# Reordering everything ahead of the experts in a two-layer decoder trunk: first loads, projection columns with Pool's mixing, added tensors, 512-wide dense products, routing, and a 0/1 scatter of the experts' results

## The reference, cut to what matters

```python
for l in range(2):
    h = rms_norm(x, mix_norm[l])
    proj = h @ w_in                                   # 3328 columns; 32 more (vres_down) in layer 1
    p_rwkv = token_shift(proj[..., :1792], mu)        # p + (prev - p) * mu; columns r, k, v (512 each), lora (256)
    p_diff = proj[..., 1792:3328]                     # q, k, v of the attention, 512 each
    ...
    y_rwkv = rwkv7_time_mix(p_rwkv, ...)              # delta-rule recurrence over 256 tokens, 8 heads of 64
    y_diff = diff_attention(p_diff, ...)
    x = x + concat(y_rwkv, y_diff) @ out_proj[l]
    x = x + memory_cross_attention(rms_norm(x), rms_norm(mem), ...)
    h = rms_norm(x, ffn_norm[l])
    x = x + (swiglu(h, dense) if l == 0 else moe_swiglu(h, router, experts))
```

## Time and profile before

| what | value |
|---|---|
| median of 3 runs | 2137.33 us (2130.75 to 2857.82) |
| the profiled execution's own time | 2133.89 us |
| its span in the trace | 2131.9 us |
| TensorE clock granted, mean | 0.961 |
| busy: PE, DVE, ACT, POOL | 92%, 76%, 60%, 5% |

### The profile page before, as it was taken

One profiled execution on the slowest core, in us unless ns is written; L12 is line 12 of the kernel. 1 busy time (PEld: TensorE's weight loads), 2 busy tenths in 40 slices (PEclk: granted clock), 3 DMA queues, 4 the chain that ended last, 5 costly groups with the idle time before them and its releaser, 6 DMA issues.

```text
span 2131.9 us, 30794 instructions
## 1 busy us (share of the span) xinstructions
PE 1957.5 (92%) x9976; PEld 1625.7 (76%) x9976; DVE 1612.9 (76%) x2233; ACT 1275.9 (60%) x1793; POOL 111.5 (5%) x95
## 2 busy tenths in 40 slices
PE   5888988879998888988869999999999999999998
PEld 4677867669996578867657878888787887878886
DVE  4786586546655676586559989898898989999897
ACT  3542374345554433374237878777787777778775
POOL 1021220000001011320000000000000000000000
PEclk8999999989998799999969999999999999999999
DMA  7430035235554330034159999999999999989994
GB/s 248 142 109 21 11 122 170 83 116 178 183 184 140 119 109 21 11 119 129 55 186 337 372 323 374 333 348 348 343 378 321 365 339 347 370 316 382 321 362 166
DMA packets 223611, 474.35 MB, mean 222 GB/s; under 512 B 15605, under 2 KB 40817, under 8 KB 223141
## 3 DMA queue, kind: packets, MB, share of 16 engines
q1 hardware_dynamic: 218064, 458.49, 61.2%
q0 software_dynamic: 1648, 9.96, 1.4%
q10 hardware_dynamic: 3813, 4.79, 0.8%
HBM read 468.44 MB, written 1.05 MB: 220 GB/s over the span
## 4 chain that ended last, share of the span: by engine, by line
PE 56%; DVE 9%; issue 2%; ACT 2%; ACTq 0%; DVEq 0%
PE psum L398 16%; PE psum L400 15%; PE psum L399 15%; PE psum L865 2%; PE psum L875 1%; PE psum L909 1%; PE psum L422 1%; DVE x L1907 1%; DVE w_lo L375 1%; DVE NB L1397 1%; DVE SH L1426 1%; DVE st L1403 1%; PE psum L591 1%; DVE w_lo L359 1%; DVE w_lo L354 0%
## 5 line engine op out<-in xcount | busy, mean ns | idle before, releaser
L398 PE MATMUL psum<-w_hi,h_hi 128*128 128x512 f32 (+1 forms) x1992 | 768.4, 386 | 51.1 <-DVE w_lo L359 30.9
L399 PE MATMUL psum<-w_lo,h_hi 128*128 128x512 f32 (+1 forms) x1992 | 747.8, 375 | 0.0
L400 PE MATMUL psum<-w_hi,h_lo 128*128 128x512 f32 (+1 forms) x1992 | 747.0, 375 | 0.0
L398 PEld LDWEIGHTS psum<-w_hi,h_hi 128*128 128x128 f32 x1992 | 384.5, 193 | 139.7 <-DVE w_lo L359 30.6
L400 PEld LDWEIGHTS psum<-w_hi,h_lo 128*128 128x128 f32 x1992 | 383.9, 193 | 67.6
L399 PEld LDWEIGHTS psum<-w_lo,h_hi 128*128 128x128 f32 x1992 | 384.6, 193 | 66.4 <-issue 4.5
L359 DVE SCALAR_TENSOR_TENSOR w_lo<-ring,col,w_hi 128x256 fp32r<-128x256 f32 (+1 forms) x320 | 169.4, 586 | 156.7 <-ACT w_hi L346 144.9
L346 ACT ACTIVATE w_hi<-ring,col 128x256 fp32r<-128x256 f32 (+1 forms) x320 | 166.6, 584 | 182.0 <-PE psum L400 171.5
L375 DVE TENSOR_TENSOR w_lo<-ring,w_hi 128x1024 fp32r<-128x1024 f32 x144 | 171.7, 1221 | 13.5 <-ACT w_hi L371 8.2
L354 DVE TENSOR_TENSOR w_lo<-ring,w_hi 128x1024 fp32r<-128x1024 f32 x86 | 106.6, 1249 | 87.5 <-ACT w_hi L341 87.1
L371 ACT ACTIVATE w_hi<-ring 128x1024 fp32r<-128x1024 f32 x144 | 151.1, 1060 | 28.7 <-PE psum L400 28.6
(11 more groups left out here) (291 smaller groups left out, 2541.8 us busy)
## 6 DMA issues: line engine op xcount, KB each, us to landing
ring<-in_expert_w_gu SPq DMA_DIRECT2D x128, 512.0 KB, 5.4
SH<-in_expert_w_gu SPq DMA_DIRECT2D x120, 512.0 KB, 5.8
proj<-in_expert_w_gu SPq DMA_DIRECT2D x104, 512.0 KB, 6.0
dproj<-in_expert_w_gu SPq DMA_DIRECT2D x72, 512.0 KB, 5.8
dproj<-in_expert_w_down SPq DMA_DIRECT2D x72, 512.0 KB, 5.0
ring<-in_expert_w_down SPq DMA_DIRECT2D x64, 512.0 KB, 5.0
ring<-in_in_proj SPq DMA_DIRECT2D x48, 512.0 KB, 4.4
ring<-in_dense_w_gu SPq DMA_DIRECT2D x44, 512.0 KB, 3.5
```

Of the source, the lines that this page charges most:

```text
L398: pe.matmul(o, h[0], w[0], start=start, stop=False, skip_group_check=True)
L399: pe.matmul(o, h[0], w[1], start=False, stop=False, skip_group_check=True)
L400: return pe.matmul(o, h[1], w[0], start=False, stop=stop, skip_group_check=True)
```

## The change

It does the following.

- **First loads:** SP issues the rest of the constants after 8 ring blocks, not 4; Pool's first loads wait for the first four ring blocks, `mus` goes out ahead of `vecs`, and the angles of the rotary embedding are computed later. PE takes the first block between the two halves of x's transposes.
- **Projection columns:** the order becomes k, lora, r, v. The shifted copies are issued by Pool. DVE mixes k and lora (and the 32 columns of `vres`), Pool mixes r and v (three 128x1024 operations each) and copies or blends v; `r_ready` and `v_ready` tell the others. DVE does the norm of k in between, with explicit `split_to` counts. The 8 blocks of r and v lie between the small products.
- **Fillers:** some `rest` and `kv` blocks are moved within the recurrence and out of the attention; the four transposes of the memory go two by two.
- **Added tensors:** before the transposes of a half of x, ACT and DVE split one or two blocks fewer (`more=-1`, `-2`), and PE takes a block between the two halves (`xq`, the dense part, layer 1's projection).
- **Dense:** blocks hold 256 rows of both gate and up (two transfers), so that the matmuls are 512 wide; a second buffer for the hidden part; the last chunk's order.
- **Routing:** `sel` and `Psel` first, the items' table after, the overflow loop on Pool.
- **Scatter:** the matrix holds only 0 and 1 (`slotT`, float32r), the result is split into `y_hi` and `y_lo`, the gate is applied in the addition.

```diff
-        mu = nbf[:, 0:NMU]
+        mu = hN[:, 0:NMU]
-        chunks_in = [(0, 512), (512, 512), (1024, 512), (1536, 256), (1792, 512), (2304, 512), (2816, 512)]
+        chunks_in = [(512, 512), (1536, 256), (0, 512), (1024, 512), (1792, 512), (2304, 512), (2816, 512)]
+        K_, LORA_, R_, V_, VR_ = range(5)
...
-                        blocks += [("gu", gu_block(dense_gu[0], c, *g), 0, (0, COL["ffn"] + 4 * g[1])) for g in GU]
+                        blocks += [("gu", gu_block(dense_gu[0], c, k0), 512, (0, COL["ffn"] + k0)) for k0 in range(0, KD, 2)]
...
+                some(in_steps, 1)
+                if l == 0:
+                    pe.wait_ge(x_in_s[1], 16)
+                    half_T(("hT", 0, 0), x, 1)
+                else:
+                    x_half(("hT", l, 0), 1, lambda g, t: ("fy", 2 * t + g))
+                some(in_steps, 7)
...
-                some(rest, 2)
+                some(in_steps, 4)
                 pe.wait_ge(lora_ready, l + 1)
                 transposes(("lt", l), ...)
...
+                some(in_steps, 2)
...
+                pe.wait_ge(small_in, 32)
+                for t in range(TT):
                     pe.wait_ge(sg_scan, TT * l + t + 1)
...
+                some(rest, 4)
...
+                    pe.wait_ge(v_ready, l + 1)
                     bank = open_work(("U", l, t))
...
-                    some(kv, 1 if h % 2 else 3)
+                    some(kv, (2, 1, 2, 1)[h])
...
+                xq_steps = project_steps(("xq", l), half_chunks(2), ("hT", l, 2))
+                some(xq_steps, 1)
                 x_half(("hT", l, 2), 1, lambda g, t: ("op", l, g, t))
...
-                    B.filled(pe.matmul(bank[:, :], PgT[:, t * P:(t + 1) * P], Ysb[:, n * 512:(n + 1) * 512], start=True, stop=True), ("sc", t, n))
+                    to, ns = slotT[:, t * P:(t + 1) * P], slice(n * 512, (n + 1) * 512)
+                    pe.matmul(bank[:, :], to, y_hi[:, ns], start=True, stop=False)
+                    B.filled(pe.matmul(bank[:, :], to, y_lo[:, ns], start=False, stop=True), ("sc", t, n))
...
+            def shift_in(l, g):
...
+                pool.dma_start(prev[1:113, :, cs], pv[0:112, :, cs]).then_inc(shifted_in[g], 16)
+                pool.dma_start(prev[113:128, :, cs], pv[112:127, :, cs]).then_inc(shifted_in[g], 16)
+                pool.dma_start(prev[0:1, 1, cs], pv[127:128, 0, cs]).then_inc(shifted_in[g], 16)
+            def mix(l, g):
+                pool.wait_ge(shifted_in[g], 48 * (l + 1))
+                c0, cw = shift_cols[g]
+                p_, q_ = pv[:, :, c0:c0 + cw], prev[:, :, c0:c0 + cw]
+                step(pool.tensor_tensor(q_, q_, p_, SUB))
+                step(pool.tensor_tensor(q_, q_, bc(mu[:, c0:c0 + cw].unsqueeze(1), TT, cw), MUL))
+                return pool.tensor_tensor(p_, p_, q_, ADD)
...
+                pool.wait_ge(sq_done, 2 * 3 * l + TT)
+                pool.dma_start(mu, mus[l].partition_broadcast(P)).then_inc(mu_in, 16)
+                shift_in(l, K_)
+                if l == 0:
+                    for w_, s in ((vresd_w[:, :, :], vres_down[0].rearrange("(k p) n -> p k n", p=P)),
+                                  (router_w[:, :, :], router[0].rearrange("(k p) n -> p k n", p=P))):
+                        pool.dma_start(w_, s).then_inc(lw_in, 16)
+                    for q in range(DEPTH):
+                        pool.dma_start(scol[:, q:q + 1], vecs[q:q + 1, a:a + w].rearrange("l p -> p l")).then_inc(scol_in, 16)
+                    pool.dma_start(vec[:, :], vecs[0].partition_broadcast(P)).then_inc(vec_in, 16)
+                shift_in(l, LORA_)
+                if l:
+                    shift_in(l, VR_)
+                pool.wait_ge(mu_in, 16 * (l + 1))
+                shift_in(l, R_)
+                mix(l, R_).then_inc(r_ready, 1)
+                shift_in(l, V_)
+                if l == 0:
+                    step(mix(l, V_))
+                    pool.tensor_copy(v_first[:, :, :], pv[:, :, 2 * RW:3 * RW]).then_inc(v_ready, 1)
+                else:
+                    step(mix(l, V_))
+                    v_, dv = pv[:, :, 2 * RW:3 * RW], hT[:, 1024:2048].rearrange("p (t c) -> p t c", t=TT)
+                    step(pool.tensor_tensor(dv, v_first[:, :, :], v_, SUB))
+                    pool.wait_ge(vmix_done, TT)
+                    step(pool.tensor_tensor(dv, dv, vmix, MUL))
+                    pool.tensor_tensor(v_, v_, dv, ADD).then_inc(v_ready, 1)
...
+                split_to(base + 9)
+                dve.wait_ge(mu_in, 16 * (l + 1))
+                next(k_mix)
+                split_to(base + 10)
+                next(k_mix)
                 dve.wait_ge(vec_in, 16 * (l + 1))
+                tt(nb(KK), k_v, bc(V("kk_s").unsqueeze(1), TT, RW), MUL)
+                split_to(base + 11)
...
+                for n in range(2):
+                    bank, ns = psum[B.use[("ey", n)][0]], slice(n * 512, (n + 1) * 512)
+                    dve.wait_ge(y_hi_done, 2 * i + n + 1)
+                    B.release(dve.tensor_tensor(y_lo[:, ns], bank[:, :], y_hi[:, ns].bitcast(F32), SUB), ("ey", n))
```

More of the change, by code:

```diff
@@ L268, in half_chunks, with gu_block @@
             return [(c * 512, 512) for c in range(n)]
[L271 to L275, removed]
+        def gu_block(w, c, k0):
+            return [rows(w, k0, g * FD + c * FC, FC) for g in range(2)]
         def down_block(w, c, k):
             return w[c * FC + k * P:c * FC + (k + 1) * P, :]
-        blocks = []
+        blocks, first_block = [], []
         for l in range(DEPTH):
+            first_block.append(len(blocks))
             blocks += square_blocks(in_proj[l], chunks_in[0:4], gain=(l, COL["mix"])) + square_blocks(in_proj[l], chunks_in[4:], gain=(l, COL["mix"]))
@@ L293, in decoder_trunk @@
         NPRE = len(blocks)
+        arrived = [16 * sum(2 if b[0] == "gu" else 1 for b in blocks[n % RING:n + 1:RING]) for n in range(NPRE)]
         STEPS = FE // FCE
@@ L811, in down @@
                                     last = down_product(c, k, t, n, both[k], k == 1)
-                                    if k == 1:
-                                        B.filled(last, ("fy", t * 2 + n))
-                                if n == 1 and k == 0:
-                                    used(last)
+                                    if n and t and k == 0:
+                                        used(last)
+                                B.filled(last, ("fy", t * 2 + n))
                         used_with(("fy", 3))
-                        work[0] += -work[0] % 4
@@ L881, in _ @@
                 bank = B.open(pe, ("ey", n), 4 + n)
-                B.filled(pe.matmul(bank[:, :], PgT[:, 0:P], Ysb[:, n * 512:(n + 1) * 512], start=True, stop=True), ("ey", n))
+                B.filled(pe.matmul(bank[:, :], no_result[:, 0:P], no_result[:, :], start=True, stop=True), ("ey", n))
             start, start_used = list(B.n), n_used[0]
@@ L1111, in _, with copy @@
             split_to, ahead = splitter(act, lambda n: hi_of(act, n))
-            def copy(dst, name, src=None, scale=1.0, func=ACT.Copy):
-                ahead(name)
+            def copy(dst, name, src=None, scale=1.0, func=ACT.Copy, more=0):
+                ahead(name, more)
                 bank = B.wait_filled(act, name)
@@ L1420, in _, with evac @@
             split_to, ahead = splitter(dve, lambda n: lo_of(dve, n))
-            def evac(dst, name, src, other, op):
-                ahead(name)
+            def evac(dst, name, src, other, op, more=0):
+                ahead(name, more)
                 bank = B.wait_filled(dve, name)
@@ new lines, in _, with mix @@
+                dve.wait_ge(mu_in, 16 * (l + 1))
+                heads = lambda a: a.rearrange("p (n c) -> p n c", c=HD)
+                kkf, bf = NB[:, KK, :], NB[:, B_, :]
+                r_v, k_v, v_v = (pv[:, :, i * RW:(i + 1) * RW] for i in range(3))
+                def mix(g):
+                    dve.wait_ge(shifted_in[g], 48 if g == VR_ else 48 * (l + 1))
+                    c0, cw = shift_cols[g]
+                    p_, q_ = pv[:, :, c0:c0 + cw], prev[:, :, c0:c0 + cw]
+                    tt(q_, q_, p_, SUB)
+                    yield
+                    tt(q_, q_, bc(mu[:, c0:c0 + cw].unsqueeze(1), TT, cw), MUL)
+                    last = dve.tensor_tensor(p_, p_, q_, ADD)
+                    if g == K_:
+                        step(last)
+                    else:
+                        last.then_inc(lora_ready, 1)
+                    yield
```

466 lines of the change are left out of this document (242 added, 224 removed).

## The result

The changed kernel takes 2074.88 us (median of 4 executions, 2073.67 to 2076.99), the kernel before in the same session 2134.87: a ratio of 0.973, 95% interval 0.9705 to 0.9748. One of the four executions of the kernel before took 2857.82 us and is left out of the ratio. That is 60 us gained where 97 were forecast; 2074.88 stands at the slow edge of the stated range (2005 to 2075), and by the ratio, 0.9726 of 2133.89, it is 2075.4. The profiled execution took 2073.67 us, its span is 2071.7.

The account below looks back on a forecast made before the run. PE bounds the kernel: ahead of the experts its holes are waits, in the experts only less PE work helps. Gains of 20, 3, 6.6, 8.6, 7.4, 18, 7.3, 13 and 13 sum to 96.9: 2133.9 to 2037 us, range 2005 to 2075.

Parts of the forecast that it names:

- Recurrence fillers: Both layers' recurrences: three more blocks within the levels would meet a hole at one level; 3 us gained, bounds -8 and 10.
- Pool as a link: Layer columns: the wait for Pool's mixed v hides behind PE's 28.5 us of other work; cost 0, bounds 0 and 10.
- second rival: Pool's mixing and DVE's small operations block each other and `v_ready` comes late; 30 us lost, 2067 us; chance 0.12.
- First loads and layer 0's columns: Start to `aT`: the wait for `mus` goes, `vec` costs 6 us; 20 us gained, bounds 12 and 28.
- P: Theory of the experiments: Pool's mixing holds DVE up, so PE's lo parts come late in both layers' columns.
- Layer 1's columns: Layer 1's projection: 8 us from holes and 10 from the clock, 18 us gained, bounds 6 and 26.
- 512-wide dense: Dense chunks: 48 wide matmuls replace 96 narrow ones; 7.3 us gained, bounds 6 and 8.
- Block between the halves: Blocks cover waits for x's halves: `xq` 6.6, dense start 8.6, dense end 7.4 us; bounds together 12 and 25.
- Routing: Logits to first expert product: h's scaling and items' table go behind, first splits ahead; 13 us gained, bounds 10 and 15.
- Scatter: Experts: four float32r matmuls of 0.91 us replace float32 products of 1.72; 13 us gained, bounds 8 and 15.
- F: Theory of the experiments: the new placement of blocks and memory transposes within the recurrences costs what these stretches got longer.
- theory D: Theory of the experiments, against Pool's mixing as cause: DVE simply has more to do in the columns than PE.

Follow-up runs that it names:

- old_fill: Changed kernel with only the placement of blocks and memory transposes inside recurrences and attention put back as before the change: 2040.24 us, ratio 0.956.

## Why the prediction was wrong, step by step

**What bounds the kernel**: right. PE sets the end, its holes are waits for DVE, and an expert stays a PE stage.

***Recurrence fillers*, +3 with bounds -8 and 10: the step that failed most.** The stretches lost 18.1 and 16.2 us net of the one block more in each. I priced each block at 2.7 us and asked only whether it met a hole. It also shifts where DVE's lo parts stand among the copies on which PE waits (124.19 and 126.26 above). With the blocks out of levels 1 and 4 the time falls by 21 us, and of the 20.4 us of layer 0's first half in old_fill only 2.9 are holes and 5.4 the blocks themselves; 12.1 go with the lower clock. Which hole brings the clock down is not shown: the same 1.67 us were followed by 16.7 us of it in one run, by 3.4 in another. I also counted the blocks that were added within the levels and put no price on the one that left its place behind U; that opened the 3.0 us of L624 in each layer. And the attention's lost cover, which I named, came to 13.4 us of waits for 4.0. My bound, "every uncovered wait comes back", left the clock out, though the earlier trace rows had shown it. Under the earlier trace rows the old recurrence ran at 0.95, so it had a clock to lose.

***Pool as a link*, 0 with bounds 0 and 10: the second.** I asked whether `v_ready` comes in time. It does: nobody waited for it. What I did not charge is Pool's mixing as a burden on DVE: 28.8 us by the run without it. The second rival had half of the mechanism. (Its 9 us a layer are four small operations, not four in each of two mixes.) Its small operations are there, in layer 0 alone: three groups lost 6.1 us beside the mix of r (7.06 in place of 0.93). It left out DVE's large operations with two tensors, which lost as much: in layer 0 4.8 us in four lo parts and 2.1 in two products of 128x1024 ahead of them, in layer 1 6.2 in six lo parts beside r alone. A late `v_ready`, 12 of its 30 us, did not come. That 30 is near 28.8 is luck. The Trainium skill (SBUF — State Buffer, "Who interferes with whom") says that a DVE instruction with two SBUF inputs contends with a Pool instruction that reads SBUF. The rows agree: 7.58 us for four lo parts in place of 2.74. Of DVE's modes that take both port pairs it says that whoever issues first has the shared pair for the whole instruction and the other blocks. The rows agree in the small operations, which end 0.03 us behind Pool's. Its remark that issue order decides who blocks fits the copy that came 0.01 us ahead of Pool's and took 0.17, and Pool's operations of up to 3.23 us beside DVE's large ones in place of 2.4; no run here changed the order alone.

***First loads and layer 0's columns*, 20**: the wait for `mus` went, and `vec` came late by 6.1 us for 6 forecast. The rest was P: without Pool's mixing `aT` comes at 102.1 in its one trace, 21.9 sooner than before against 22.7 forecast.

***Layer 1's columns*, with *dense end* and *512-wide dense***: 30.7 of 35.4, and 10.5 more without Pool's mixing.

***Block between the halves***: undersized. To the first dense product 19.0 us were gained for 11.9: the holes of that stretch went from 23.9 to 10.3, and its clock from 0.93 to 0.97. About 1 us of the 19.0 is moved, not gained: the second half's transposes now stand behind the first dense product. Here the clock worked for the change (as an estimate, 0.07 of 125.2 us less 0.03 of 106.2, 5.6 us), and I had charged the holes alone.

***512-wide dense***: the chunks stand 16.8 us apart for 16.7 forecast:

```profile
455.89 0.60 PE L821 MATMUL psum<-cst,NB 128*128 128x128 f32 x4
...
472.69 0.60 PE L821 MATMUL psum<-cst,NB 128*128 128x128 f32 x4
```

***Routing*, 13**: 14.7. ***Scatter*, 13**: right in itself; an expert takes 123.90 us, not 124.7. The four matmuls take what was forecast, 0.93 us against 0.91:

```profile
1098.86 0.39 PE L914 MATMUL psum<-y_hi,slotT 128*128 128x512 f32 x1
...
1099.79 0.40 PE L423 MATMUL psum<-w_hi,h_hi 128*128 128x512 f32 x1
```

An old one has the same 1.72 us from start to full pace in the third expert as in the earlier trace rows, so two scatters give 1.6 of the 2.43 us an expert. The other 0.8 lie in short gaps between ordinary products, of which the new expert's trace has fewer:

```profile
1384.55 0.39 PE L400 MATMUL psum<-w_hi,h_lo 128*128 128x512 f32 x1
1384.98 0.50 PE L398 MATMUL psum<-w_hi,h_hi 128*128 128x512 f32 x1
```

Here, in the kernel before, 0.43 us lie between two starts that are 0.23 apart at pace. What made these gaps stays open. The transfers' share is 0.98 in the new expert and caps nothing.

Set against the forecast of 96.9: columns and dense part -19.4, recurrences -37.4, the two stretches behind them +10.5, routing and experts +9.6, which leaves the 60 measured. With F undone and the mixing of r and v on DVE, the kernel takes 2025 against 2037 forecast; that is not the forecast's kernel, and its nearness to 2037 proves no single term.

**The range** was drawn too tight by its own words: two thirds of the way from 2037 to 2098 is 2078, not 2075. And the upper bound of the fillers, half of a hole of 20.0 us in each layer, is 20, not 10.

## What to carry to other kernels

Moving element-wise work to an idle Pool is not free where DVE's output is what PE waits for: look in the trace for DVE operations that end just behind Pool's, and compare one of them with its duration elsewhere. If so, either give DVE the work (14.6 us of it cost 14.0 here, where Pool's mixing cost 28.8) or cut Pool's operations small; reordering DVE's own list gained nothing that stands clear of the spread. Before adding filler work to a chain of short dependent steps, price the clock as well as the hole, and try each place by itself: here moving two blocks a layer out of the levels gave 21 us, and undoing the memory pairs, which headed the waits there, nothing.

## What the runs showed of the hardware that I had not expected

- The lower clock outlasts the wait before it: after a wait of 1.67 us it stayed for 16.7 us of full work in one run; the same hole in the run without r's and v's mixing was followed by 3.4 us of it. Why the length differs stays open: no run here changed the hole alone.
- Cutting Pool's operations into four moved part of the cost from DVE to Pool (DVE's busy time up to `aT` 78.8 to 74.4 us, Pool's mix of r 7.3 to 11.8), although both do the same work. How the turns are given was not tried further.
- DVE's busy time contains its waits for Pool: 78.8 us in layer 0's columns with Pool's mixing, 66.6 without. A busy share alone would have spoken for theory D.
